# Output projection of a gated hybrid layer: where a weight sum is made, who splits it, and what the merges read

## The chip, the cores and the metric

One NeuronCore of a Trainium2 chip. The metric is the device time of one execution of the whole program, in microseconds (us); several executions are taken and their median is used.

## The reference

One layer on 512 tokens of width 1024, all in float32. A wide input projection feeds two token mixers (a gated linear recurrence and a top-k sparse attention). Only the end of the layer matters here:

```python
ua = einsum('blc,cd->bld', oa * silu(za), w_up_a)      # 512 -> 1024
ub = einsum('blc,cd->bld', ob * silu(zb), w_up_b)      # 512 -> 1024
merged = sigmoid(ga) * ua + sigmoid(gb) * ub
y = einsum('bld,de->ble', merged, w_out)               # 1024 -> 1024
return layer_norm(ALPHA * x + y, ln_g, ln_b)
```

## The kernel before

**Precision.** Every float32 product is made of three matmuls on rounded operands: high by high, high by low, low by high. So every weight tile is loaded by SP's DMA queue, rounded to a high part by ACT (`round_tiles` L965, `split_out_hi` L1213), and the low part, raw minus high, is made by POOL (`split_lo` L1984, `split_out_lo` L2058, a quarter of a weight at a time, 128x512) or in some places by DVE.

**Order of the work.** The program walks units of weights (`UNITS`, L54). A unit is four quarters q, q = 4u to 4u+3, and one quarter is 12 matmuls of 128x512. Units 0 to 26 are the input projection, units 27 to 30 (`up0` to `up3`, q = 108 to 123) the two up projections. Each engine has its own in-order program, written out by quarter: the same q in two engines' loops is only a place in each list, and semaphores tie them. Constants give the places: `T1_AT` and `T1_LO_AT` (DVE), `OUT_HI_AT` (ACT), `OUT_LO_AT` (POOL).

**Up projections and merges.** Two quarters give the two products of 128 channels m (0 to 7), in two of four PSUM banks (`up_bank`). Before a quarter may write its bank again, PE waits until the bank's earlier content was read (`quarter_up`, L717, semaphores `up_out`). `merge(m)` on DVE (L1708) multiplies one bank by its gate into an SBUF tile `mix` (L1719), the other by its gate (L1720), adds the two from SBUF (L1723), waits until ACT has rounded the sum (`round_merged`, L1192), and takes the low part (L1726). After each odd m, `sum_rows` (L1736 to L1743) makes four short differences of 128x256 for the products below, ACT rounds them (`round_sums`, L1197), and DVE makes their low part (`sum_rows_lo`, L1749).

**Output projection.** It is done as a 2x2 block product with seven block products in place of eight. Their weights are, in PE's order (`OUT_WEIGHTS`): `b11`, `b21`, `t1`, `t2`, `b22`, `t3`, `t4`, where t1 = b12 - b11, t2 = b22 - t1, t3 = b22 - b12, t4 = b21 - t2 (`sum_out`, L1770, one DVE instruction of 128x2048 each). Each block product is two passes i of four steps j, three matmuls a step. A step waits for its quarter of the weight's low part (`wait_out_lo`) and, in `b11`, `b21` and `t1`, for the low part of its activations: `b11` step 3 needs merge 6, `b21` step 3 merge 7, `t1` step 3 the last `sum_rows_lo`. `b21` adds to the banks of `b11`, so its pass i waits until ACT has kept a copy (`keep_first`, L1218).

**Where the raw blocks lie.** SP loads `b11` into `z_a` and `b12` into `z_b` behind the weights of `up1`, after `o_lo_done` (both tiles hold branch outputs until then). t1 is written over `b11` in `z_a`, so it waits for `b11`'s low part; its low part is one DVE instruction (`first_sum_lo`, L1776) at q = 121; t2 then overwrites t1, t3 overwrites `b12`. `b21` and `b22` come into the two halves of `w_raw` when the last up weights are split.

**Tail.** DVE adds residuals and partial results in the PSUM banks (`rows_11`, `early_rows`, `rows_12`, `rows_22`), makes the row statistics, and normalises; SP stores the result. `rows_12(i)` frees the banks for `b22`.

Of the kernel before, what the change touches and what calls it, by code (L numbers as in the profile page):

```python
# [93 lines left out]
LO_DVE = tuple(range(Q_PREP[0] // 4 + 1, Q_MERGE // 4 + 2))  # L94
OUT_HI_AT = {109: ((0, 0),), 110: ((0, 1),), 117: ((1, 0),), 118: ((1, 1),), 120: ((2, 0), (2, 1))}
OUT_LO_AT = {110: 0, 119: 1}
T1_AT, T1_LO_AT = 115, 121
ON_POOL = ((), (1,), (1,), ())
# [16 lines left out]
def hybrid_kernel(nc, x_t, x_tok, w_units, w_kiwi, b_cols, b_ia, b_vb, lb_cols, g_cols, rel_bias,  # L115
                  ln_g, ln_b, one_hot, ident, causal, tree_masks, out):
    with ExitStack() as ctx:
# [355 lines left out]
        def out_raw(name):  # L473

            u2, u3 = UNITS.index("up2"), UNITS.index("up3")
            ring = {"b21": u2, "t4": u2, "b22": u3}
            if name in ring:
                return w_raw[:, ring[name] % 2, :].rearrange("p (j n) -> p j n", j=PAIRS)
            return z_a[:] if name in ("b11", "t1", "t2") else z_b[:]

# [6 lines left out]

        LO_ORDER = (0, 1, 4, 3, 5, 6)

        def wait_out_lo(eng, n, pieces):  # L490

            if n == 2:
                eng.wait_ge(out_lo_dve, 1)
            else:
                eng.wait_ge(out_lo, 4 * LO_ORDER.index(n) + pieces)

# [61 lines left out]
        def _(sp):  # L558
# [20 lines left out]
            sp.dma_start(id_sb[:], ident).then_inc(early_in, 16)  # L579
            def load_out(name):  # L580
                sp.dma_start(out_raw(name), w_units[NMAIN - 1 + OUT_BLOCKS.index(name)]
                             .rearrange("p (j n) -> p j n", j=PAIRS)).then_inc(out_in[name], 16)

            for u in range(2, NMAIN):
                if u >= 3:
                    wait_lo(sp, u - 2, 4)
                for a in range(2):
                    load_half(u, a)
                if u == 3:
                    for dst, src in ((lb[:, 0, :], lb_cols), (g_a[:], g_cols), (causal_sb[:], causal),  # L590
                                     (masks_sb[:], tree_masks), (bias_ia[:], b_ia.partition_broadcast(P)),
                                     (bias_vb[:], b_vb.partition_broadcast(P))):
                        sp.dma_start(dst, src).then_inc(consts_in, 16)
                    sp.wait_ge(table_done, 1)
                    sp.dma_start(t5_row, table[:]).then_inc(row_out, 16)
                if u in (10, 14):
                    both_halves((10, 14).index(u))
                if u == 5:
                    sp.wait_ge(row_out, 16)
                    slid = bass.AP(t5_row.tensor, t5_row.offset, [[1, P], [T5W, HEADS_B], [1, 2 * P]])  # L600
                    sp.dma_start(t5_turned[:], slid).then_inc(t5_in, 16)
                if UNITS[u] == "up1":
                    sp.wait_ge(o_lo_done, 4)
                    load_out("b11")
                    load_out("b12")
            sp.wait_ge(recur_done, HEADS_A)
            sp.dma_start(ln_gb[:, 0, :], ln_g.partition_broadcast(P)).then_inc(ln_in, 16)
            sp.dma_start(ln_gb[:, 1, :], ln_b.partition_broadcast(P)).then_inc(ln_in, 16)
            wait_lo(sp, UNITS.index("up2"), 4)
            load_out("b21")  # L610
            wait_lo(sp, UNITS.index("up3"), 4)
            load_out("b22")
            sp.wait_ge(part_done, parts(UNITS.index("up3"), 1))
# [11 lines left out]
        def _(pe):  # L625
# [91 lines left out]
            def quarter_up(u, i, j):  # L717

                fill = 2 * (2 * int(UNITS[u][2]) + i) + j
                if fill < 2:  # L720
                    wait_log_out(pe, TREE0 + 2 * NTREE - 2 + fill)
                    pe.wait_ge(o_hi_done, 2 * (j + 1))
                    pe.wait_ge(o_lo_done, 2 * (j + 1))
                elif fill < 4:
                    wait_turn_out(pe, len(ITEMS) + HEADS_A - 4 + fill)
                else:
                    pe.wait_ge(up_out[fill % 4], fill // 4)
                c = slice(i * P, i * P + P)
# [199 lines left out]
            for n, i in OUT_ORDER:  # L928
# [9 lines left out]
                elif name == "t2":  # L938
                    pe.wait_ge(up_out[i], 2 * KT // 4)
                elif name == "t3":  # L940
# [22 lines left out]
        def _(act):  # L963
# [256 lines left out]
            def move_u(i):  # L1220

                act.wait_ge(up_out[2 + i], 2 * KT // 4)
                act.wait_ge(u_done, i + 1)
                nc.scalar.activation(c21_bank[i][:], u_sum[:, i, :], ACT.Copy).then_inc(u_moved, 1)
# [82 lines left out]
            for q in range(4 * NMAIN):  # L1307
# [39 lines left out]
                if m is not None:  # L1347
                    round_merged(m)
                    if m % 2:
                        round_sums(m // 2)  # L1350
            split_out_hi(4, 0)
            split_out_hi(4, 1)
            round_merged(KT - 1)
            keep_first(0)
            round_sums(PAIRS - 1)
            keep_first(1)
            for n in (3, 5, 6):
# [13 lines left out]
        def _(dve):  # L1371
# [336 lines left out]
            def merge(m):  # L1708
# [43 lines left out]
            def sum_out(name):  # L1752

                dst = out_raw(name)
                if name == "t1":
                    wait_out_raw(dve, "b11")
                    wait_out_raw(dve, "b12")
                    wait_out_lo(dve, 0, 4)
                    a, b = out_raw("b12"), out_raw("b11")
                elif name == "t2":  # L1760
                    wait_out_raw(dve, "b22")
                    dve.wait_ge(out_lo_dve, 1)
                    a, b = out_raw("b22"), out_raw("t1")
                elif name == "t3":
                    a, b = out_raw("b22"), out_raw("b12")
                else:
# [205 lines left out]
        def _(pool):  # L1972
# [95 lines left out]
            for q in range(4 * NMAIN):  # L2068
                side(q)
                if q in OUT_LO_AT:  # L2070
                    for piece in range(4):
                        split_out_lo(OUT_LO_AT[q], piece)
            for n in LO_ORDER[2:]:
                for piece in range(4):
# [75 lines left out]
```

## Time and profile before

| | |
|---|---|
| three executions | median 463.41 us (463.39 to 463.68) |
| the profiled execution | 463.86 us, its span 461.9 us, 1.96 us around it |
| busy share of the span | PE 97%, DVE 69%, ACT 51%, POOL 40% |
| mean granted TensorE clock | 0.988 of full speed |
| chain that ended last | PE 84%, DVE 9%, POOL 2%, ACT 2% |

All times of the profile count from the span's start. A row of a timeline has start, duration, engine, line and operation, output<-inputs with their shapes, the number merged into it, and in brackets the engine's idle time before it and what ended it. A matmul's own duration overlaps with the next one's: read PE by the distance of the starts. `bank` is a PSUM tile, all other names are in SBUF.

### The profile page before, as it was taken

To read this page: it belongs to the slowest core of one execution; us is meant where nothing else is said; L and a number is where in the kernel's file an instruction comes from. 1 tells how busy PE (TensorE), PEld (TensorE's weight loads), DVE (VectorE), ACT (ScalarE), POOL (GpSimd) and SP (SyncE) were. 2 spreads that over 40 slices of the span, in tenths; PEclk is the share of its full clock that TensorE was granted. 3 is DMA by queue.
4 is the path that set the end of the run, shared out by engine and by line. 5 is a ranking of instruction groups with operands and counts; after the bars stand their busy time and mean duration, and the time that the engine had idled before them with its cause. 6 is when DMAs were issued, how large, how long until landed. Compare 5 with 4: busy or idle time off the path is not lost.

```text
span 461.9 us, 7700 instructions
## 1 busy us (share of the span) xinstructions
PE 448.9 (97%) x2946; PEld 365.5 (79%) x2946; DVE 319.4 (69%) x585; ACT 236.7 (51%) x398; POOL 185.3 (40%) x173
## 2 busy tenths in 40 slices
PE   9999999999999999999999999999999999979993
PEld 7778888888888888888888887887888888757782
DVE  4446589999999843447989975960720079789977
ACT  5735454263346655376697485725873523534421
POOL 0444442582259724571013000000074486535972
PEclk9999999999999999999999999999999999988998
DMA  8808222266024620214020312050136352240013
GB/s 265 285 17 291 74 76 92 91 159 206 0 92 106 172 88 1 92 27 157 1 92 3 122 67 89 3 184 0 58 125 258 107 182 93 91 180 3 0 45 136
DMA packets 16724, 47.73 MB, mean 103 GB/s; under 512 B 2441, under 2 KB 4273, under 8 KB 16177
## 3 DMA queue, kind: packets, MB, share of 16 engines
q1 hardware_dynamic: 16448, 47.05, 30.6%
q8 instruction: 23, 0.38, 0.3%
q10 hardware_dynamic: 240, 0.20, 0.2%
q14 instruction: 13, 0.10, 0.1%
HBM read 43.04 MB, written 2.11 MB: 98 GB/s over the span
## 4 chain that ended last, share of the span: by engine, by line
PE 84%; DVE 9%; POOL 2%; issue 2%; ACT 2%; DVEq 0%; POOLq 0%
PE bank L627 21%; PE bank L628 21%; PE bank L629 20%; PE bank L788 2%; PE bank L773 2%; POOL w_lo L2058 2%; PE bank L871 2%; PE bank L824 2%; DVE s_lo L1749 1%; DVE z_a L1770 1%; DVE mix L1723 1%; PE bank L764 1%; PE bank L763 1%; PE bank L954 1%; PE bank L957 1%
## 5 line engine op out<-in xcount | busy, mean ns | idle before, releaser
L1984 POOL TENSOR_TENSOR w_lo<-w_raw,w_hi 128x512 fp32r<-128x512 f32 x84 | 113.1, 1373 | 160.0 <-ACT w_hi L965 160.0
L627 PE MATMUL bank<-x_hi,w_hi 128*128 128x512 f32 x336 | 133.0, 396 | 0.0
L628 PE MATMUL bank<-x_lo,w_hi 128*128 128x512 f32 x336 | 131.2, 390 | 0.0
L629 PE MATMUL bank<-x_hi,w_lo 128*128 128x512 f32 x336 | 130.9, 390 | 0.0
L627 PEld LDWEIGHTS bank<-x_hi,w_hi 128*128 128x128 f32 x336 | 63.1, 188 | 13.9 <-issue 0.8
L629 PEld LDWEIGHTS bank<-x_hi,w_lo 128*128 128x128 f32 x336 | 63.1, 188 | 13.6
L628 PEld LDWEIGHTS bank<-x_lo,w_hi 128*128 128x128 f32 x336 | 63.1, 188 | 12.1
L965 ACT ACTIVATE w_hi<-w_raw 128x1024 fp32r<-128x1024 f32 (+2 forms) x63 | 62.4, 1011 | 7.2 <-PE bank L629 4.1
L1052 ACT ACTIVATE prob<-prob,nmax 128x128 f32<-128x128 f32 (+3 forms) x32 | 17.7, 555 | 41.5 <-DVE nmax L1505 41.5
L1481 DVE MAX8 best<-score 128x8 f32<-128x256 f32 (+2 forms) x48 | 26.8, 559 | 1.0
L1493 DVE COPY prob_t<-bank 128x128 f32<-128x128 f32 (+3 forms) x32 | 14.2, 486 | 19.0 <-PE bank L773 18.9
L1482 DVE MATCH_REPLACE8 score<-best,score 128x256 f32<-128x256 f32 (+2 forms) x48 | 26.0, 543 | 0.0
L627 PE MATMUL bank<-o_hi,w_hi 128*128 128x512 f32 x64 | 25.1, 393 | 0.8 <-DVE mix L1719 0.8
L627 PE MATMUL bank<-w_hi,x_hi 128*128 128x512 f32 x64 | 25.3, 395 | 0.0
L629 PE MATMUL bank<-w_hi,x_lo 128*128 128x512 f32 x64 | 25.0, 390 | 0.0
L628 PE MATMUL bank<-w_lo,x_hi 128*128 128x512 f32 x64 | 24.9, 390 | 0.0
L629 PE MATMUL bank<-o_hi,w_lo 128*128 128x512 f32 x64 | 24.9, 389 | 0.0
L628 PE MATMUL bank<-o_lo,w_hi 128*128 128x512 f32 x64 | 24.9, 389 | 0.0
L1719 DVE TENSOR_TENSOR mix<-bank,gate_a_hi 128x512 f32<-128x512 f32 x4 | 2.7, 686 | 31.7 <-PE bank L629 31.7
L1042 ACT ACTIVATE relus<-bank 128x256 f32<-128x256 f32 (+2 forms) x24 | 10.5, 490 | 21.0 <-PE bank L753 21.0
L2002 POOL TENSOR_TENSOR logit<-t,pen 128x256 f32<-128x256 f32 x24 | 17.4, 742 | 9.1 <-DVE nmax L1505 9.1
L1471 DVE SCALAR_TENSOR_TENSOR score<-relus,w_idx,score 128x256 f32<-128x256 f32 (+2 forms) x21 | 15.6, 744 | 7.7 <-ACT relus L1042 6.0
(269 smaller groups left out, 846.6 us busy)
## 6 DMA issues: line engine op xcount, KB each, us to landing
w_raw<-in_w_units SPq DMA_DIRECT2D x58, 512.0 KB, 4.6
w_raw<-in_w_units SPq DMA_DIRECT2D x2, 1024.0 KB, 4.7
y_sb<-in_x_tok SPq DMA_DIRECT2D x4, 512.0 KB, 4.9
out<-y_sb SPq DMA_DIRECT2D x8, 256.0 KB, 2.0
x_raw_hi<-in_x_t SPq DMA_DIRECT2D x4, 256.0 KB, 4.5
x_raw_lo<-in_x_t SPq DMA_DIRECT2D x4, 256.0 KB, 6.4
t_turned<-t_row SPq DMA_DIRECT2D x1, 1024.0 KB, 9.8
q_hi_g<-q_hi_g SPq DMA_DIRECT2D x8, 128.0 KB, 3.7
```

The source lines that it names most:

```text
L627: nc.tensor.matmul(dst, a_hi, b_hi, start=first, stop=False)
L628: nc.tensor.matmul(dst, a_hi, b_lo, start=False, stop=False)
L629: return nc.tensor.matmul(dst, a_lo, b_hi, start=False, stop=last)
L965: nc.scalar.activation(split_target(u, kiwi_hi, x_hi, w_hi)[:, k, :], raw(u)[:, k, :], ACT.Copy).then_inc(done, 1)
L1042: nc.scalar.activation(relus[:, i % 2, 0:n], log_bank[i % 2][:, 0:n], ACT.Relu, scale=QSCALE).then_inc(log_out[i % 2], 1)
L1052: nc.scalar.activation(prob[:, i % 4, 0:n], prob[:, i % 4, 0:n], ACT.Exp, bias=nmax[:, i % 4:i % 4 + 1], scale=-1.0, accum_out=prob_sum[:, ...
L1471: ins = nc.vector.scalar_tensor_tensor(out=score[b][:], in0=relus[:, i % 2, 0:n], scalar=w, in1=score[b][:], op0=ALU.mult, op1=ALU.add)
L1481: link(nc.vector.max(best8[:], score[b][:]))
L1482: link(nc.vector.match_replace(score[b][:], best8[:], score[b][:], TAKEN))
L1493: nc.vector.tensor_copy(prob_t[:, i % 4, 0:n], turn_bank[i % 2][:, 0:n]).then_inc(turn_out[i % 2], 1)
L1984: nc.gpsimd.tensor_tensor(split_target(u, kiwi_lo, x_lo, w_lo)[:, k, :], raw(u)[:, k, :], split_target(u, kiwi_hi, x_hi, w_hi)[:, k, :].bi ...
L2002: nc.gpsimd.tensor_tensor(logit[:, i % 2, n - band:n], t5[:, h, 2 * P - band:], pen[b][:, n - band:] if b else causal_sb[:], ALU.add).then ...
```

## The change

- t1 is made at q = 106 (T1_AT 115 before), ahead of the up projections. For that SP loads `b11` and `b12` ahead of the weights of `up0`, t1 goes into `z_b` over `b12`, and SP loads `b12` once more, into `z_a`, when `b11`'s low part is there.
- t1's low part is made half by DVE, half by POOL (two pieces behind `b21`'s at q = 121).
- `merge` writes its first product back into its PSUM bank, and the add reads it there. PE's next writer of that bank waits for the add (`mix_done`) in place of the first multiply.
- ACT rounds merge 4 before the two halves of `b21`, and keeps both `b11` copies before the last `round_sums`.

```diff
-OUT_HI_AT = {109: ((0, 0),), 110: ((0, 1),), 117: ((1, 0),), 118: ((1, 1),), 120: ((2, 0), (2, 1))}
-OUT_LO_AT = {110: 0, 119: 1}
-T1_AT, T1_LO_AT = 115, 121
+OUT_HI_AT = {109: ((0, 0),), 110: ((0, 1),), 120: ((2, 0), (2, 1))}
+OUT_HI_THEN = {118: ((1, 0), (1, 1))}
+OUT_LO_AT = {110: ((0, 0), (0, 1), (0, 2), (0, 3)), 119: ((1, 0), (1, 1), (1, 2), (1, 3)), 121: ((2, 2), (2, 3))}
+T1_AT, T1_LO_AT = 106, 121
...
-            return z_a[:] if name in ("b11", "t1", "t2") else z_b[:]
+            return z_a[:] if name in ("b11", "t3") else z_b[:]
...
             for u in range(2, NMAIN):
+                if UNITS[u] == "up0":
+                    sp.wait_ge(o_lo_done, 4)
+                    load_out("b11", z_a[:])
+                    load_out("b12", z_b[:])
                 if u >= 3:
                     wait_lo(sp, u - 2, 4)
...
-                if UNITS[u] == "up1":
-                    sp.wait_ge(o_lo_done, 4)
-                    load_out("b11")
-                    load_out("b12")
...
+            wait_out_lo(sp, 0, 4)
+            sp.wait_ge(out_sum, 1)
+            load_out("b12", z_a[:])
             wait_lo(sp, UNITS.index("up2"), 4)
...
-                else:
-                    pe.wait_ge(up_out[fill % 4], fill // 4)
+                elif fill % 2:
+                    pe.wait_ge(up_out[fill % 4], fill // 4)
+                else:
+                    pe.wait_ge(mix_done, fill // 2 - 1)
...
-                    pe.wait_ge(up_out[i], 2 * KT // 4)
+                    pe.wait_ge(mix_done, KT)
+                    pe.wait_ge(up_out[1], 2 * KT // 4)
...
+                for n, half in OUT_HI_THEN.get(q, ()):
+                    split_out_hi(n, half)
...
             keep_first(0)
+            keep_first(1)
             round_sums(PAIRS - 1)
-            keep_first(1)
...
-                nc.vector.tensor_tensor(mx, up_bank[fa][:], gate_tiles(m, 1)[:, 0, :], ALU.mult).then_inc(up_out[fa], 1)
+                a_gated = up_bank[fa][:]
+                nc.vector.tensor_tensor(a_gated, a_gated, gate_tiles(m, 1)[:, 0, :], ALU.mult).then_inc(a_done, 1)
                 nc.vector.tensor_tensor(gb, up_bank[fb][:], gb, ALU.mult).then_inc(up_out[fb], 1)
-                dve.wait_ge(up_out[fa], m // 2 + 1)
+                dve.wait_ge(a_done, m + 1)
                 dve.wait_ge(up_out[fb], m // 2 + 1)
-                nc.vector.tensor_tensor(mx, mx, gb, ALU.add).then_inc(mix_done, 1)
+                nc.vector.tensor_tensor(mx, a_gated, gb, ALU.add).then_inc(mix_done, 1)
...
                 if name == "t1":
-                    wait_out_lo(dve, 0, 4)
-                    a, b = out_raw("b12"), out_raw("b11")
+                    a, b = z_b[:], z_a[:]
                 elif name == "t2":
                     wait_out_raw(dve, "b22")
-                    dve.wait_ge(out_lo_dve, 1)
-                    a, b = out_raw("b22"), out_raw("t1")
+                    wait_out_lo(dve, 2, 4)
+                    a, b = out_raw("b22"), z_b[:]
...
-                hi, lo = out_weights(2)
-                nc.vector.tensor_tensor(lo, out_raw("t1"), hi.bitcast(F32), ALU.subtract).then_inc(out_lo_dve, 1)
+                hi, lo = (w[:, 0:2, :] for w in out_weights(2))
+                nc.vector.tensor_tensor(lo, out_raw("t1")[:, 0:2, :], hi.bitcast(F32),
+                                        ALU.subtract).then_inc(out_lo_dve, 1)
...
-            for n in LO_ORDER[2:]:
+            for n in LO_ORDER[3:]:
                 for piece in range(4):
                     split_out_lo(n, piece)
```

## Rows read from the trace of the kernel before

**Rows 1.** Who waited for whom, engine PE, whole span: us, times, longest.

```profile
PE bank L954 <- DVE even_lo L1726: 2.8, 1, 2.8
PE bank L627 <- DVE mix L1719: 0.8, 1, 0.8
PE bank L954 <- ACT first_sum L1218: 0.6, 1, 0.6
PE bank L954 <- POOL w_lo L2058: 0.3, 1, 0.3
```

**Rows 2.** Timeline of PE from 403 us to the first step of t2.

```profile
403.04 0.50 PE L627 MATMUL bank<-o_hi,w_hi 128*128 128x512 f32 x1 [0.85 <-DVE mix L1719]
...
409.76 0.39 PE L957 MATMUL bank<-x_hi,even_lo 128*128 128x512 f32 x1
...
410.44 0.39 PE L957 MATMUL bank<-x_hi,even_lo 128*128 128x512 f32 x1
413.65 0.80 PE L954 MATMUL bank<-x_hi,even_hi 128*128 128x512 f32 x1 [2.83 <-DVE even_lo L1726]
...
414.67 0.63 PE L957 MATMUL bank<-x_hi,even_lo 128*128 128x512 f32 x1
415.10 0.63 PE L954 MATMUL bank<-x_hi,even_hi 128*128 128x512 f32 x1
...
431.83 0.39 PE L954 MATMUL bank<-w_hi,s_hi_hi 128*128 128x512 f32 x1
```

**Rows 3.** Stretches: busy and count by engine, PEclk (granted clock), DMA share, GB/s.

```profile
412.90:413.10 0.20, 0.00 (x0) 0.00 (x0) 0.00 (x0) 0.20 (x2) 0.00 (x0) 0.64 1.11 287
...
419.60:419.80 0.20, 0.20 (x2) 0.10 (x2) 0.20 (x1) 0.00 (x0) 0.20 (x1) 0.54 0.00 0
```

**Rows 4.** Timeline of DVE from 336 us to its last instruction.

```profile
336.77 1.75 DVE L1704 TENSOR_TENSOR o_lo<-z_b,o_hi 128x1024 fp32r<-128x1024 f32 x1 [0.48 <-ACT o_hi L1337]
...
369.34 0.69 DVE L1719 TENSOR_TENSOR mix<-bank,gate_a_hi 128x512 f32<-128x512 f32 x1 [30.83 <-PE bank L629]
...
378.49 1.50 DVE L1736 TENSOR_TENSOR s_raw<-mix 128x256 f32<-128x256 f32 x1
379.92 0.41 DVE L1737 TENSOR_TENSOR s_raw<-mix 128x256 f32<-128x256 f32 x1
...
386.98 3.37 DVE L1770 TENSOR_TENSOR z_a<-z_b,z_a 128x2048 f32<-128x2048 f32 x1
...
399.48 0.67 DVE L1726 TENSOR_TENSOR even_lo<-mix,even_hi 128x256 fp32r<-128x256 f32 x1 [2.28 <-ACT even_hi L1192]
...
403.69 1.63 DVE L1723 TENSOR_TENSOR mix<-mix,g_b 128x512 f32<-128x512 f32 x1
...
408.41 2.29 DVE L1776 TENSOR_TENSOR w_lo<-z_a,w_hi 128x2048 fp32r<-128x2048 f32 x1
...
410.61 0.69 DVE L1719 TENSOR_TENSOR mix<-bank,gate_a_lo 128x512 f32<-128x512 f32 x1
...
412.00 0.69 DVE L1723 TENSOR_TENSOR mix<-mix,g_b 128x512 f32<-128x512 f32 x1
...
414.65 0.69 DVE L1719 TENSOR_TENSOR mix<-bank,gate_a_lo 128x512 f32<-128x512 f32 x1
...
421.82 2.28 DVE L1770 TENSOR_TENSOR z_a<-w_raw,z_a 128x2048 f32<-128x2048 f32 x1
...
449.16 0.70 DVE L1817 TENSOR_TENSOR bank<-bank,y_sb 128x512 f32<-128x512 f32 x1 [0.76 <-PE bank L957]
...
458.33 0.75 DVE L1829 SCALAR_TENSOR_TENSOR y_sb<-bank,rstd,ln_gb 128x512 f32<-128x512 f32 x1
```

**Rows 5.** Timeline of POOL, the low parts of b21 and of t2.

```profile
399.82 6.65 POOL L2058 TENSOR_TENSOR x_lo<-w_raw,x_hi 128x512 fp32r<-128x512 f32 x4
...
425.29 9.13 POOL L2058 TENSOR_TENSOR w_lo<-z_a,w_hi 128x512 fp32r<-128x512 f32 x4 [4.79 <-ACT w_hi L1213]
```

**Rows 6.** DMA issues from 320 us on: KB each, median us to landing.

```profile
z_b<-in_w_units SPq DMA_DIRECT2D x1, 1024.0 KB, 9.1
```

More of the change, by code:

```diff
@@ L298, in hybrid_kernel @@
         out_sum, out_hi, out_lo, out_lo_dve = (sem(n) for n in ("out_sum", "out_hi", "out_lo", "out_lo_dve"))
+        a_done = sem("a_done")
         first_kept, pre_12, pre_21 = sem("first_kept"), sem("pre_12"), sem("pre_21")
@@ L486, in wait_out_raw @@
                 eng.wait_ge(out_sum, ("t1", "t2", "t3", "t4").index(name) + 1)
-        LO_ORDER = (0, 1, 4, 3, 5, 6)
+        LO_ORDER = (0, 1, 2, 4, 3, 5, 6)
         def wait_out_lo(eng, n, pieces):
+            before = 4 * LO_ORDER.index(n) - 2 * (LO_ORDER.index(n) > LO_ORDER.index(2))
             if n == 2:
                 eng.wait_ge(out_lo_dve, 1)
+                if pieces > 2:
+                    eng.wait_ge(out_lo, before + pieces - 2)
             else:
-                eng.wait_ge(out_lo, 4 * LO_ORDER.index(n) + pieces)
+                eng.wait_ge(out_lo, before + pieces)
         HI_ORDER = (0, 1, 2, 4, 3, 5, 6)
@@ L579, in _, with load_out @@
             sp.dma_start(id_sb[:], ident).then_inc(early_in, 16)
-            def load_out(name):
-                sp.dma_start(out_raw(name), w_units[NMAIN - 1 + OUT_BLOCKS.index(name)]
+            def load_out(name, dst):
+                sp.dma_start(dst, w_units[NMAIN - 1 + OUT_BLOCKS.index(name)]
                              .rearrange("p (j n) -> p j n", j=PAIRS)).then_inc(out_in[name], 16)
             for u in range(2, NMAIN):
+                if UNITS[u] == "up0":
+                    sp.wait_ge(o_lo_done, 4)
+                    load_out("b11", z_a[:])
+                    load_out("b12", z_b[:])
                 if u >= 3:
@@ L608, in _ @@
             sp.dma_start(ln_gb[:, 1, :], ln_b.partition_broadcast(P)).then_inc(ln_in, 16)
+            wait_out_lo(sp, 0, 4)
+            sp.wait_ge(out_sum, 1)
+            load_out("b12", z_a[:])
             wait_lo(sp, UNITS.index("up2"), 4)
-            load_out("b21")
+            load_out("b21", out_raw("b21"))
             wait_lo(sp, UNITS.index("up3"), 4)
-            load_out("b22")
+            load_out("b22", out_raw("b22"))
             sp.wait_ge(part_done, parts(UNITS.index("up3"), 1))
@@ L1220, in move_u @@
             def move_u(i):
-                act.wait_ge(up_out[2 + i], 2 * KT // 4)
                 act.wait_ge(u_done, i + 1)
@@ L1757, in sum_out @@
                     wait_out_raw(dve, "b12")
-                    wait_out_lo(dve, 0, 4)
-                    a, b = out_raw("b12"), out_raw("b11")
+                    a, b = z_b[:], z_a[:]
                 elif name == "t2":
                     wait_out_raw(dve, "b22")
-                    dve.wait_ge(out_lo_dve, 1)
-                    a, b = out_raw("b22"), out_raw("t1")
+                    wait_out_lo(dve, 2, 4)
+                    a, b = out_raw("b22"), z_b[:]
                 elif name == "t3":
-                    a, b = out_raw("b22"), out_raw("b12")
+                    dve.wait_ge(out_in["b12"], 32)
+                    a, b = out_raw("b22"), z_a[:]
                 else:
@@ L2069, in _ @@
                 side(q)
-                if q in OUT_LO_AT:
-                    for piece in range(4):
-                        split_out_lo(OUT_LO_AT[q], piece)
-            for n in LO_ORDER[2:]:
+                for n, piece in OUT_LO_AT.get(q, ()):
+                    split_out_lo(n, piece)
+            for n in LO_ORDER[3:]:
                 for piece in range(4):
```

## The prediction, made before the changed kernel was run

> **What bounds the kernel now.** I read the busy shares first: PE is busy 97% of the span, so the only time to win is what PE loses. PE's waits [rows 1] say where: except at the start, all lie behind 401 us, in the last up projection and the output projection. In PE's timeline [rows 2] three matmuls take 0.68 us (409.76 to 410.44), one 0.227. Against that distance I count the losses: 1.1 us around 403.04, where a bank waits for merge 5's first multiply (0.1 of it a hiccup before); 3.0 us before 413.65, where `b11` step 3 waits for the low part of merge 6; 0.8 and 0.4 us where `b21` waits for ACT's second copy and `t2` for POOL's low part [rows 1]. The long wait also lowers the clock: it is granted in full until 412.9, stands at half (1.2 of 2.4 GHz) from 413.1, and comes back at 419.8 [rows 3]. PE runs 15 matmuls in there at 0.43 us (414.67 to 415.10, [rows 2]): 15 x 0.2 = 3.0 us. Together 8.3 us of PE time, and no change here can win more.
>
> Why is merge 6 late? Its products are there at 369.3 + 6 x 5.44 = 401.9 (merge 0 starts at 369.34 straight behind PE, two quarters are 24 matmuls or 5.44 us), and DVE begins it at 410.61 [rows 4]. DVE is 8.7 us behind, so from merge 2 to the sum t2 its queue is the bound, with ACT and POOL woven in. The end hangs on DVE too: from the last residual step behind `t3` (449.16) DVE runs without a gap until 459.08 [rows 4], and the store follows. That part isn't touched; it starts when PE has done `t3`. So the gain is what PE reaches `t3`'s end earlier.
>
> **One mechanism prices most steps.** The same 128x2048 subtraction takes 3.37 us at 386.98 and 2.28 at 421.82; the add from two SBUF tiles takes 1.63 at 403.69 and 0.69 at 412.00; a 128x256 step takes 1.50 at 378.49 and 0.41 right behind it [rows 4]. The slow ones are those that start while POOL is inside a piece. Steps with one input in PSUM are 0.69 throughout. I read it as a lock: a DVE step with two SBUF inputs waits out POOL's piece, up to 1.09 us, and POOL waits out DVE's step. While both have work they alternate.
>
> **DVE's queue up to merge 6, term by term.**
> - t1's sum leaves: 3.37 less 0.08 of overlap, -3.3 [rows 4]. At q = 106 DVE is idle (30.8 us before 369.34), so there it costs nothing; it may hold a POOL piece by 2.3 us, and the piece belongs to unit 26's weights and ends near 351, and PE takes them from 353.0 on.
> - Merge 4's low part waited 2.28 us for ACT, which had two halves of `b21` ahead of it (row 399.48). Now ACT rounds merge 4 first; the normal wait of some 0.5 and a lock wait of up to 0.7 stay: -1.1.
> - The adds read PSUM and take no lock: merge 5's -0.94 (1.63 against 0.69), merges 0 and 1 -0.8 by letting POOL finish sooner. No more, since merge 2 can't start before its products at 380.2.
> - t1's low part on DVE is halved, 2.29 to about 1.2: -1.1. POOL gets two pieces, 2.5 us.
> - New lock waits. POOL began `b21`'s low part at 399.82 and ended at 406.47 [rows 5], before the short sums of merge 5. DVE now comes to that merge's low part at about 400 and the sums at 401, with POOL still at `b21` and then at t1's pieces until 405: +0.5 for the low part and three of the four sums at 1.09, +3.8.
>
> Sum: -3.3 - 1.1 - 0.94 - 0.8 - 1.1 + 3.8 = -3.4. Merge 6 starts at 407.2 and its low part is there at about 410.0. Merge 7: 414.65 becomes 411.2. Its add stood in a lock wait too (-0.94), half of it comes back at the low part behind it: t2's sum ends 3.9 us earlier, at 420.2 in place of 424.1.
>
> **PE's side, as a second sum.** The wait at 403 goes: merge 5's add ends at about 399.4, and PE wants the bank at 401.9. PE begins `b11` at 407.5 and comes to step 3 at 409.6: a wait of 0.5 us in place of 3.0, too short to lower the clock (the 0.85 us one at 403.04 didn't). `b11` ends at 413.5. Then `b21` waits for `keep_first(0)`, which stands behind merge 7's rounding at 413.5: 0.9 us in place of 0.8. So PE is at `t2` at 425.3, 6.5 us earlier than before (431.8, [rows 2]). But `t2`'s low part is only 3.9 us earlier: POOL's four pieces took 9.13 us, because t3's and t4's sums on DVE come between them [rows 5]. The last piece ends at 430.5, and PE wanted it at 427.3: 3.2 us of waits, the longest, for the third piece, about 2.5. After: 0.5 + 0.9 + 3.2 = 4.6 us lost in place of 8.3: -3.7. The two sums agree, and I take **-3.8 us**: DVE's queue gives 3.9, and what is left over is POOL's `t2` wait.
>
> **Costed at nothing.** The early loads: the two blocks can go out at 338.5, when the last branch part is split (336.77 + 1.75, [rows 4]), and `up0`'s weights land behind them. Before, `b12` landed 9.1 us after issue as the last of 3 MB [rows 6]; so all is there by about 350, and ACT rounds `up0`'s weights in unit 26, which begins at 369.3 - 16.3 = 353.0. The third load (1 MB, about 376 to 381) is wanted by t3's sum at 421; `b21` and `b22` follow it on SP's queue, at 386 and later. The two `ln` loads stand ahead of SP's new wait. PE's waits for `mix_done`: odd quarters keep theirs, and each even one has 2 us or more (above). Writing a product back to PSUM: steps that write a bank (row 449.16, 0.70) cost what the others do. The add from PSUM, in any case, by its nearest rows: 0.69 with a bank as input (410.61), 0.69 without (412.00) [rows 4]; for the read just behind the write I allow 0 to 0.1 us a merge.
>
> A page speaks against this step. The Trainium skill, "VectorE: DVE Perf Modes", section on the TRN2 errata, gives a PSUM source 120 fixed cycles and an SBUF source 58, which would be 0.065 us more for each add, 0.3 us over the five merges on the path (an estimate from that page). The rows above don't agree: both forms take 0.69.
>
> **Rivals.**
> 1. *The wait moves and takes the clock along (28%).* The new wait at `t2`, about 2.5 us, lies between the one that left the clock alone (0.85) and the one before 413.65, in which it fell 2.1 us after PE's last matmul had ended (410.83, [rows 2, 3]). So a fall is near even. It costs 0.2 us a matmul; a spell as long as before is 3.0 us, one of half the length 1.5. The time is -3.8 + 1.5 to 3.0: 461.1 to 462.6 by the runs. Then the gain was in the first stall and half of it is paid again at `t2`.
> 2. *DVE and POOL don't alternate step by step (15%).* After the slow 378.49 the next sum was 0.41, but POOL had just run out of pieces. If only the first sum waits, 2.2 us come back, and with the POOL pieces for `t2` as much again at most: 455.8 to 458.
> 3. *The savings are eaten by lock waits (8%).* The two extra POOL pieces meet DVE where it is densest, and two more waits of 1.09 and a late phase bring merge 6 to its old place: `b11` waits and loses the clock again, 463 to 463.9.
> 4. *Slower: banks held until the add (6%).* The point is the quarter at 401.9, which now waits for merge 5's add and not its first multiply. With DVE as late as before (add ending 405.3) PE stands 3.4 us there, loses the clock (3.0) and begins `b11` at 413.9, when its low part is just ready; the old wait of 3.0 and spell of 3.0 are gone, so it is no change until the add ends after 405.6, and from there every us counts: two lock waits more are +2.2, 465.5. Against it: the add ends at 399.4 by the sum above, 6 us before the point.
>
> That the change does not do what it says is no rival with weight: DVE and SP are idle where t1 is put.
>
> **The numbers.** The profiled execution is 463.86, 0.45 above the median of the runs, 463.41. 463.86 - 3.8 = 460.1 for a profiled one; against the median 459.6. The forecast's own chance is 43%, its own range 458.3 to 460.7. The range that holds 8 in 10 reaches from 457.4 (most of rival 2) to 462.5 (rival 1 up to a full spell); rivals 3 and 4 and the far end of 2 are left out. A measurement of this kernel tells apart about 0.2%, 0.93 us. Faster by more: forecast, nearly all of rival 1, rival 2: 0.84. Within: rival 3 and the edge of 1: 0.10. Slower: 0.06.
>
> **What the profile would show.** Right: no PE wait near 403; `b11` step 3 waits under 1 us and the clock stays full around 413; the adds at L1723's place are 0.7 every time; the sums of merge 5 show 1.4 to 1.5 in several of the four steps; merge 6 starts near 407, merge 7 near 411, t2's sum ends near 420; PE's largest wait is `t2` for POOL's low part. Wrong: sums of 0.41 there and merge 6 near 404 (rival 2); half clock near 430 (rival 1); merge 6 after 410 (rival 3); a PE wait for merge 5's add (rival 4). A DVE gap of over 10 us between `t3` and the end would break the step that carries the gain to the end.

## The result and the profile after

The changed kernel takes **460.66 us** (median of 4 executions, 459.87 to 461.21) against 463.43 (463.39 to 463.68): a ratio of 0.9938, 95% interval 0.9921 to 0.9955, so 2.8 us less. The prediction was 459.6, with a range of 457.4 to 462.5 and 0.84 for faster. A second measurement of the same kernel gave 461.57 (6 executions, 0.9944, 0.9927 to 0.9962). The profiled execution took 459.87 us, its span is 457.8 us, 4.1 less than before.

From the page of after: the span, PE's busy share, the granted clock in 40 slices.

```profile
span 457.8 us, 7703 instructions
...
PE 445.2 (97%) x2946; PEld 362.8 (79%) x2946; DVE 319.7 (70%) x585; ACT 236.7 (52%) x398; POOL 186.3 (41%) x175
...
PEclk9999999999999999999999999999999999999997
```

Only the last slice, behind the matmuls, is below full clock. Who waited for whom on PE, after (us, times, longest), answering to [rows 1]:

```profile
PE bank L965 <- POOL w_lo L2072: 2.6, 2, 2.3
...
PE bank L965 <- DVE even_lo L1739: 1.0, 1, 1.0
PE bank L965 <- ACT first_sum L1229: 0.5, 1, 0.5
```

The largest wait has changed its place: not `b11` for DVE's low part of merge 6 (2.8 before), but `t2` for POOL. The wait at 403 is gone. PE's timeline of after, answering to [rows 2]:

```profile
409.96 0.50 PE L965 MATMUL bank<-x_hi,even_hi 128*128 128x512 f32 x1 [0.98 <-DVE even_lo L1739]
...
414.23 0.50 PE L965 MATMUL bank<-x_hi,odd_hi 128*128 128x512 f32 x1 [0.54 <-ACT first_sum L1229]
...
425.24 0.39 PE L965 MATMUL bank<-w_hi,s_hi_hi 128*128 128x512 f32 x1
...
429.07 0.50 PE L965 MATMUL bank<-w_hi,s_hi_lo 128*128 128x512 f32 x1 [2.28 <-POOL w_lo L2072]
...
430.32 0.50 PE L965 MATMUL bank<-w_hi,s_hi_lo 128*128 128x512 f32 x1 [0.29 <-POOL w_lo L2072]
```

`t2` begins at 425.24 in place of 431.83, 6.6 us earlier, and gives 2.6 back at once. The chain of work that ended last passes this place in both kernels: it comes from DVE over `t2`'s four low parts on POOL to PE's matmul behind the last of them, at 430.32 here. Before, that matmul was (POOL's row in [rows 5] ends at 434.42)

```profile
434.47 0.50 PE L954 MATMUL bank<-w_hi,s_hi_lo 128*128 128x512 f32 x1 [0.27 <-POOL w_lo L2058]
```

PE's wait at `b11` and its half clock before are not in that chain: PE came to `t2`'s last piece 0.27 us too early even so.

DVE's timeline of after, answering to [rows 4]:

```profile
345.36 2.74 DVE L1783 TENSOR_TENSOR z_b<-z_b,z_a 128x2048 f32<-128x2048 f32 x1 [7.30 <-DMA z_b<-in_w_units]
368.89 0.70 DVE L1732 TENSOR_TENSOR bank<-bank,gate_a_hi 128x512 f32<-128x512 f32 x1 [20.79 <-PE bank L637]
...
398.21 0.69 DVE L1736 TENSOR_TENSOR mix<-bank,g_b 128x512 f32<-128x512 f32 x1
399.60 1.51 DVE L1739 TENSOR_TENSOR odd_lo<-mix,odd_hi 128x512 fp32r<-128x512 f32 x1 [0.70 <-ACT odd_hi L1203]
401.04 1.50 DVE L1749 TENSOR_TENSOR s_raw<-mix 128x256 f32<-128x256 f32 x1
402.47 1.51 DVE L1750 TENSOR_TENSOR s_raw<-mix 128x256 f32<-128x256 f32 x1
403.90 1.51 DVE L1753 TENSOR_TENSOR s_raw<-s_raw,mix 128x256 f32<-128x256 f32 x1
405.44 0.43 DVE L1756 TENSOR_TENSOR s_raw<-mix,s_raw 128x256 f32<-128x256 f32 x1
405.78 1.22 DVE L1789 TENSOR_TENSOR w_lo<-z_b,w_hi 128x1024 fp32r<-128x1024 f32 x1
406.92 0.69 DVE L1732 TENSOR_TENSOR bank<-bank,gate_a_lo 128x512 f32<-128x512 f32 x1
...
410.95 0.69 DVE L1732 TENSOR_TENSOR bank<-bank,gate_a_lo 128x512 f32<-128x512 f32 x1
...
417.71 2.28 DVE L1783 TENSOR_TENSOR z_b<-w_raw,z_b 128x2048 f32<-128x2048 f32 x1
...
445.04 0.70 DVE L1831 TENSOR_TENSOR bank<-bank,y_sb 128x512 f32<-128x512 f32 x1 [0.76 <-PE bank L968]
...
454.21 0.75 DVE L1843 SCALAR_TENSOR_TENSOR y_sb<-bank,rstd,ln_gb 128x512 f32<-128x512 f32 x1
```

The adds are 0.69 throughout, and three of merge 5's four short sums take 1.5 us, though a sum of this size takes 0.41: I read it as alternation with POOL (experiment 6 tests it). POOL's rows for the low parts of `b21`, t1's two pieces and t2 [rows 5] are now

```profile
395.79 6.47 POOL L2072 TENSOR_TENSOR x_lo<-w_raw,x_hi 128x512 fp32r<-128x512 f32 x4
402.22 2.90 POOL L2072 TENSOR_TENSOR w_lo<-z_b,w_hi 128x512 fp32r<-128x512 f32 x2
...
421.17 9.10 POOL L2072 TENSOR_TENSOR w_lo<-z_b,w_hi 128x512 fp32r<-128x512 f32 x4 [4.79 <-ACT w_hi L1224]
```

**One offset first.** Merge 0 begins at 369.34 before and at 368.89 after. Among the twelve profiles of this study it lies between 368.39 and 369.44, and in two profiles of the changed kernel alone it is 368.89 and 369.30. So I don't count the 0.45 of the 4.1 us as the edit's, and below I count DVE's times from merge 0. Counted so, they repeat within 0.02 us in the two profiles of the changed kernel, up to where PE's clock differs (431 us).

### The profile page after: what moved, and what is told of

It is laid out like the page before. It is cut to its first block, busy times and chain, and to the rows that moved or that the text cites. A ratio compares the mean times of both kernels' runs of the same rounds, so it can differ in the third digit from the quotient of the medians.

```text
span 457.8 us, 7703 instructions
## 1 busy us (share of the span) xinstructions
PE 445.2 (97%) x2946; PEld 362.8 (79%) x2946; DVE 319.7 (70%) x585; ACT 236.7 (52%) x398; POOL 186.3 (41%) x175
## 4 chain that ended last, share of the span: by engine, by line
PE 85%; DVE 9%; POOL 2%; issue 2%; ACT 2%; DVEq 0%; POOLq 0%
PE bank L635 21%; PE bank L636 21%; PE bank L637 21%; PE bank L798 2%; PE bank L783 2%; POOL w_lo L2072 2%; PE bank L881 2%; PE bank L834 2%; DVE s_lo L1762 1%; PE bank L774 1%; PE bank L773 1%; PE bank L965 1%; PE bank L968 1%; PE bank L967 1%; PE bank L925 1%
## 5 line engine op out<-in xcount | busy, mean ns | idle before, releaser
L1697 DVE TENSOR_TENSOR w_lo<-w_raw,w_hi 128x512 fp32r<-128x512 f32 x32 | 20.6, 684 | 0.0
```

The lines of the kernel that those rows point to most:

```text
L1697: nc.vector.tensor_tensor(split_target(u, kiwi_lo, x_lo, w_lo)[:, k, :], raw(u)[:, k, :], split_target(u, kiwi_hi, x_hi, w_hi)[:, k, :].bi ...
```

## The experiments

My theory, after this reading: the gain comes from DVE's queue up to merge 6, which PE's order then follows; the lock between DVE and POOL (a DVE step with two inputs in SBUF and a POOL piece exclude each other) sets both the three slow sums and the late third piece of t2; and the median is above the profiled execution because the clock falls in PE's wait at `t2` in some executions. The rivals: that the early sum t1 alone did it; that the add from PSUM is worth only its own 0.94 us; that sharing t1's low part pays.

Places in each profile, in us from merge 0, worked out from the timelines: the start of DVE's merges 3, 5 and 6, the end of t2's sum on DVE, the start of PE's last matmul; then merge 5's four short sums, and where the profile shows the clock at half ahead of the last matmul:

| kernel | merge 3 | merge 5 | merge 6 | t2 sum | last matmul | merge 5's sums | half clock |
|---|---|---|---|---|---|---|---|
| before | 20.93 | 32.97 | 41.27 | 54.76 | 84.76 | 0.41 0.41 0.41 0.42 | at `b11` |
| after | 17.04 | 27.94 | 38.03 | 51.10 | 81.09 | 1.50 1.51 1.51 0.43 | none |
| `after_again` | 17.05 | 27.93 | 38.02 | 51.10 | 82.38 | 1.51 1.51 1.51 0.43 | at `t2` |
| `sbuf_add` | 17.62 | 29.36 | 39.91 | 53.41 | 83.36 | 1.51 1.51 1.51 0.43 | none |
| `t1_late` | 19.24 | 30.03 | 40.12 | 53.20 | 84.08 | 1.50 1.51 1.51 0.42 | at `t2` |
| `pool_hold` | 17.03 | 27.93 | 35.83 | 48.92 | 78.87 | 1.51 0.41 0.41 0.42 | none |
| `lo_on_dve` | 17.03 | 27.93 | 36.89 | 49.96 | 81.52 | 1.50 0.41 0.41 0.42 | at `t2` |
| `before_psum_add` | 19.24 | 31.28 | 39.13 | 52.19 | 82.18 | 0.41 0.41 0.41 0.43 | none |
| `before_act_order` | 20.94 | 31.73 | 41.14 | 54.64 | 84.60 | 1.51 0.41 0.41 0.42 | at `b11` |
| `rows_first` | 17.03 | 27.95 | 38.04 | 51.10 | 78.96 | 1.51 1.51 1.51 0.42 | none |
| `both` | 17.03 | 27.95 | 35.86 | 48.96 | 76.78 | 1.50 0.41 0.41 0.42 | none |
| `lo_rows` | 17.05 | 27.94 | 36.90 | 49.97 | 77.83 | 1.50 0.41 0.41 0.42 | none |

One regularity is worth more than the medians. From the end of t2's sum to the last matmul it takes 29.95 to 30.00 us in six profiles, whatever PE waited for at `b11` and `b21`, and whether or not the clock fell at `b11`. Where the clock fell at `t2` it takes 0.9 to 1.6 more (31.28, 30.88, 31.56), and in the three kernels with the rows first 27.82 to 27.86. So a part of the change is worth what it does to t2's sum, and a fall of the clock costs time at `t2` and none at `b11`.

**1. `after_again`: the changed kernel once more.**

> The changed kernel once more, unaltered, to see its spread. Theory A (the gain is 3.7 to 4.1 us with the clock full throughout, and in some executions the clock falls in the 2.3 us wait ahead of t2's third quarter and up to 2 us are given back): 459.6 to 461.4 again, a spread of over 0.8 us where before has 0.3, and if the profile falls on a slow one it shows half clock near 430 us. Rival B (the spread comes from the early part of the kernel, as loads): a slow profile shows full clock near 430 and merge 0 later than 369.4.

Six executions: 459.55, 459.72, 461.55, 461.59, 461.83, 461.99, with nothing between; the upper four are up to 0.6 above the expected range. The profiled one is 461.55. Stretches of it: busy time and count of PE, PEld, DVE, ACT, POOL, then the granted clock, DMA share and GB/s; then PE's timeline.

```profile
429.00:429.50 0.50, 0.01 (x1) 0.02 (x1) 0.50 (x1) 0.50 (x2) 0.50 (x2) 1.00 0.00 0
430.00:430.50 0.50, 0.50 (x2) 0.01 (x1) 0.47 (x2) 0.34 (x1) 0.50 (x1) 0.71 0.00 0
431.00:432.00 1.00, 1.00 (x3) 0.81 (x4) 0.97 (x3) 0.00 (x0) 1.00 (x2) 0.50 0.00 0
433.50:434.00 0.50, 0.50 (x4) 0.41 (x3) 0.34 (x1) 0.24 (x1) 0.50 (x1) 0.88 0.00 0
```

```profile
429.49 0.49 PE L965 MATMUL bank<-w_hi,s_hi_lo 128*128 128x512 f32 x1 [2.26 <-POOL w_lo L2072]
...
430.73 0.79 PE L965 MATMUL bank<-w_hi,s_hi_lo 128*128 128x512 f32 x1 [0.19 <-POOL w_lo L2072]
...
433.45 0.47 PE L965 MATMUL bank<-w_hi,s_hi_hi 128*128 128x512 f32 x1
...
451.68 0.39 PE L968 MATMUL bank<-x_hi,odd_lo 128*128 128x512 f32 x1
```

The wait is the same to 0.02 us (2.26 here, 2.28 in the first profile), but here the clock stands at 1.2 of 2.4 GHz from about 430.2 to 433.6, and there it stays full. The first profile's stretch, and its last matmul, are

```profile
431.00:432.00 1.00, 1.00 (x6) 0.82 (x5) 0.97 (x3) 0.00 (x0) 1.00 (x2) 1.00 0.00 0
...
449.98 0.39 PE L968 MATMUL bank<-x_hi,odd_lo 128*128 128x512 f32 x1
```

From the third piece to the last matmul PE needs 22.19 us here (451.68 - 429.49) and 20.91 there (449.98 - 429.07): the fall costs 1.28 us. So rival 1's mechanism and the forecast's are both true, of different executions of one program. For the executions without a profile only the mean clock is on record: 0.990 to 0.991 in three of the upper four, 0.994 in the fourth (461.59), in both of the lower ones and in all of the first set (459.87 to 461.21). It doesn't settle them, since a fall at the end of the program, where no matmul is left, lowers the mean as well. That the fall makes the whole spread is therefore not shown.

**2. `sbuf_add`: the change without the adds from PSUM.**

> The changed kernel with the merges adding from SBUF again, PE waiting for the first multiply. Theory A (an add from SBUF waits out a POOL piece, up to 1.09 us, and holds POOL off): merge 5's add ends 2.4 us later, near 401, merge 6's low part near 411.4, t2's sum 2.4 us later near 422.4: 462.5 to 463.2, b11's wait 2.6 us in place of 1.0, the clock perhaps down there. Rival (the lock wait only changes places, since POOL's pieces are the same number): within 0.5 us of the changed kernel, 460.2 to 461.2.

```diff
-                a_gated = up_bank[fa][:]
-                nc.vector.tensor_tensor(a_gated, a_gated, gate_tiles(m, 1)[:, 0, :], ALU.mult).then_inc(a_done, 1)
+                nc.vector.tensor_tensor(mx, up_bank[fa][:], gate_tiles(m, 1)[:, 0, :], ALU.mult).then_inc(up_out[fa], 1)
...
-                nc.vector.tensor_tensor(mx, a_gated, gb, ALU.add).then_inc(mix_done, 1)
+                nc.vector.tensor_tensor(mx, mx, gb, ALU.add).then_inc(mix_done, 1)
```

(and the waits of PE, ACT and DVE as they were before the change). 462.91 us (12 executions, 461.70 to 464.27; 0.9988, 0.9976 to 1.0001), as expected: most of the gain is gone. Merge 5 in its timeline:

```profile
400.00 1.65 DVE L1733 TENSOR_TENSOR mix<-mix,g_b 128x512 f32<-128x512 f32 x1
402.35 1.01 DVE L1736 TENSOR_TENSOR odd_lo<-mix,odd_hi 128x512 fp32r<-128x512 f32 x1 [0.70 <-ACT odd_hi L1200]
```

The add is held 0.96, and in turn holds POOL, so the low part behind it gets 0.50 back. Merge 6 is 1.88 later than in after, t2's sum 2.31, and PE waits 2.9 at `b11` again.

**3. `before_psum_add`: the kernel before with that part alone.** The same edit the other way round.

> The kernel before with one part of the change: the merges keep the first product in its PSUM bank, add from there, and PE waits for the add. Theory A (each add then takes no lock and doesn't hold POOL): merge 6's low part 2.3 us earlier, b11's wait 1.2 us in place of 2.8 and the clock up there, t2's sum 2.8 us earlier: 460.8 to 461.8, single executions up to 463 where the clock falls at t2. Rival (the adds gain only the two slow ones on the path, 1.9 us, and the clock still falls at b11): 462 to 463. Rival (PE's wait for the add costs more than the lock): 463.6 or more, with a longer PE wait near 402.

461.34 us (5 executions, 460.94 to 461.82; 0.9953, 0.994 to 0.9966): -2.25, nearly all that the whole change brings. Merge 6 comes 2.14 earlier and t2's sum ends 2.57 earlier. That is far more than one add's 0.94: t1's sum too takes 2.28 here in place of 3.37, because POOL is done sooner, so part of what the forecast booked under t1's sum comes with the adds. The wait before `b11` step 3 is 0.9 in place of 2.8, and the clock stays full there; but the last matmul comes 2.58 earlier, just as much as t2's sum, so the clock adds nothing to it. PE's waits (first and third of the view):

```profile
PE bank L958 <- ACT first_sum L1222: 2.7, 2, 2.2
...
PE bank L958 <- DVE even_lo L1730: 0.9, 1, 0.9
```

and in ACT's timeline the reason for the first:

```profile
419.42 1.06 ACT L1201 ACTIVATE s_hi_lo<-s_raw 128x1024 fp32r<-128x1024 f32 x1 [3.64 <-DVE s_raw L1747]
420.38 0.58 ACT L1222 ACTIVATE first_sum<-bank 128x512 f32<-128x512 f32 x1
```

The second copy of `b11` stands behind the rounding of the last sums, and PE waits 2.16 us for it. In the changed kernel, which has `keep_first(1)` ahead, that wait is gone; but no time hangs on it here, since PE then still waits 0.30 at `t2` for POOL.

**4. `before_act_order`: the kernel before with ACT's order of the change alone.**

```diff
-OUT_HI_AT = {109: ((0, 0),), 110: ((0, 1),), 117: ((1, 0),), 118: ((1, 1),), 120: ((2, 0), (2, 1))}
+OUT_HI_AT = {109: ((0, 0),), 110: ((0, 1),), 120: ((2, 0), (2, 1))}
+OUT_HI_THEN = {118: ((1, 0), (1, 1))}
...
+                for n, half in OUT_HI_THEN.get(q, ()):
+                    split_out_hi(n, half)
...
             keep_first(0)
+            keep_first(1)
             round_sums(PAIRS - 1)
-            keep_first(1)
```

> The kernel before with another part alone: ACT rounds merge 4 ahead of b21's halves, and keeps both b11 copies ahead of the last rounding of sums. Theory A (DVE then comes 1.7 us earlier to merge 5, but meets POOL's b21 pieces, and gives it all back in lock waits): 463.0 to 463.7, no change; merge 6 starts at 410.2 to 410.6. Rival (it gives its 1.1 us and the 0.8 of b21): 461.5 to 462.3.

463.31 us (12 executions, 462.77 to 465.21, three of them above 464.8; 1.0001, 0.999 to 1.0012): nothing. Merge 5 does begin 1.24 earlier (32.97 to 31.73), as the step had it (-1.1); but DVE then meets POOL still inside `b21`'s pieces, one short sum takes 1.51 in place of 0.41, merge 6 is 0.13 earlier, and t2's sum 0.12. What the three slow executions had, no profile shows. Time won in front of a lock is spent at it.

**5. `t1_late`: the change with t1's sum at its old place.** One edit: `T1_AT` 115 in place of 106.

> The changed kernel with t1's sum back at q = 115, between the merges; all else stays. Theory A (DVE is behind there, but part of the 2.2 us is slack before merge 4 and 5): t2's sum ends 1.9 us later, 461.7 to 462.6, b11's wait about 2.5 us. Rival (the early sum is the whole gain, 3.3 us): 463.4 or more. Rival (DVE's queue there is hidden): 460.7.

462.98 us (12 executions, 461.91 to 464.18; 0.9986, 0.9976 to 0.9996): 0.4 above the range, so a miss. The sum itself is quick there:

```profile
386.19 2.28 DVE L1783 TENSOR_TENSOR z_b<-z_b,z_a 128x2048 f32<-128x2048 f32 x1
```

2.28 us in place of 3.37 before, and merge 6 is 2.09 later than in after. What I had left out is the clock: PE waits 3.02 for merge 6, where it stays full, and 2.28 at `t2`, where the profile has it at half at 432 to 433. That fall costs 0.9 (30.88 us from t2's sum to the last matmul, for 30.0), and 463.12 less 0.9 would be in the range. The spread is 2.3 us, but the mean clocks of the executions (0.987 to 0.994) don't order their times, so what makes it isn't settled.

**6. `pool_hold`: POOL's pieces of t1's low part wait until the sums of merge 5 are made.**

```diff
             def split_out_lo(n, piece):
 
+                if n == 2:
+                    pool.wait_ge(s_raw_done, 12)
                 name = OUT_WEIGHTS[n]
```

> The changed kernel with POOL's two pieces of t1's low part held back until DVE has made the four short sums of merge 5. Theory A (those pieces cost DVE two lock waits of 1.09 us, and they aren't wanted before 419): two of the three 1.5 us sums at 401 to 405 shrink to 0.4, merge 6 starts near 404.9, b11 does not wait, t2's sum ends near 417.9: 2.1 us faster than the changed kernel, 458.2 to 459.2. Rival (the sums wait for POOL whatever is in its queue, or POOL is then late for t1): no gain, 460.2 to 461.5.

457.95 us (4 executions, 457.71 to 458.24; 0.9878, 0.9865 to 0.989), 0.25 better than the expected range. DVE's and POOL's rows:

```profile
401.58 1.51 DVE L1749 TENSOR_TENSOR s_raw<-mix 128x256 f32<-128x256 f32 x1
403.01 0.41 DVE L1750 TENSOR_TENSOR s_raw<-mix 128x256 f32<-128x256 f32 x1
403.34 0.41 DVE L1753 TENSOR_TENSOR s_raw<-s_raw,mix 128x256 f32<-128x256 f32 x1
```

```profile
404.29 3.46 POOL L2074 TENSOR_TENSOR w_lo<-z_b,w_hi 128x512 fp32r<-128x512 f32 x2 [1.49 <-DVE s_raw L1756]
```

Two sums went from 1.51 to 0.41, 2.20 together, and merge 6 is 2.20 earlier; up to merge 5 nothing moved (27.93 for 27.94). POOL stood idle for 1.49 and nobody needed its pieces. This is the lock by itself, with its price: 1.10 us for each of the two sums that met a piece.

**7. `lo_on_dve`: t1's low part wholly on DVE, in one 128x2048 step.** The kernel after with POOL's two pieces left out and the DVE step over all of `w_lo`.

> The changed kernel with t1's low part made by DVE alone again, as in the kernel before. Theory A (sharing it costs more than it gives: POOL's two pieces cost two lock waits of 1.09 us and save 1.1 us of DVE): merge 6 starts 1 us earlier, near 405.9, b11 waits under 0.3 us, t2's sum 1 us earlier: 458.9 in executions without a fall of the clock, median 458.7 to 460.5. Rival (the share pays, as it frees DVE by 1.1 us): 461.2 to 462.5.

460.08 us (5 executions, 459.31 to 460.55; 0.9924, 0.9913 to 0.9936). The DVE step is 2.28 in place of 1.22, two sums 0.41 in place of 1.51: -2.20 + 1.06 = -1.14, and the table has merge 6 at 36.89 for 38.03. So the sharing that the change brings in costs more than it saves. The clock falls at `t2` in its profile (460.55) and costs 1.6; the two executions with a mean clock of 0.994 are 459.31 and 459.75, the three at 0.991 are 460.08 to 460.55. Without a fall I had expected 458.9, so the lowest is 0.4 above that.

**8. `rows_first`: DVE's statistics and early residual steps ahead of the sums t3 and t4.** The wait left in all kernels built on the change is `t2` for POOL, whose four pieces take 9.1 us because t3's and t4's sums come between. This kernel puts other DVE work there.

```diff
-            sum_out("t3")
             dve.wait_ge(ln_in, 32)
             rows_11(0)
-            sum_out("t4")
             rows_11(1)
             early_rows(0)
+            sum_out("t3")
+            rows_12(0)
             early_rows(1)
-            rows_12(0)
             rows_12(1)
+            sum_out("t4")
```

(on ACT, `move_u` goes ahead of the rounding of t4).

> The changed kernel with DVE's order behind t2's sum altered: the two b21 row steps and the first of t1's ahead of t3's sum, and t4's sum behind rows_12; ACT moves the partial sums ahead of rounding t4. Theory A (t2's low part on POOL is late only because t3's and t4's sums come between its pieces): the four pieces take about 5 us in place of 9.1, PE's 2.3 us wait at t2 goes, and with it the falls of the clock: 456.3 to 457.5, spread under 0.5 us. Rival (DVE's work there is a bound of its own and t4's sum is now late): 458.5 to 460.5, with a new PE wait at b22 or t4.

457.90 us (4 executions, 457.70 to 458.00; 0.9878, 0.9865 to 0.9891). The pieces now run without a hold, and PE's waits have no POOL at `t2`:

```profile
421.15 5.04 POOL L2074 TENSOR_TENSOR w_lo<-z_b,w_hi 128x512 fp32r<-128x512 f32 x4 [4.79 <-ACT w_hi L1224]
```

```profile
PE bank L965 <- DVE even_lo L1741: 1.0, 1, 1.0
PE bank L965 <- DVE bank L1803: 0.7, 1, 0.7
```

From t2's sum to the last matmul it is 27.86 us in place of 29.99. The time is 0.4 above the expected range: t4's sum (3.23 at 432.23) now stands ahead of `b22`'s statistics, DVE waits 0.93 for `rstd` behind ACT's rounding of t4, and PE 0.7 for a partial bank. The spread of these four is 0.3 us; but in `pool_hold`, which keeps a wait of 2.19 at `t2`, it is 0.5, so that the missing wait is what narrows it is not shown.

**9. `both`: 6 and 8 together.**

> Both rearrangements of the kernel after at once: GpSimd's pieces of t1's low part held back until DVE has made all the sums for b21, b22 and b12, and DVE's statistics and early rows ahead of the sums of t3 and t4. If the two savings lie at different places of the path (lock alternation ahead of merge 6, the wait for t2's third piece behind b21), they add up: each kernel alone measured 457.95 and 457.90, against 459.6 of the kernel after where its clock does not fall, so 1.65 and 1.7 off, together 3.35 off: 455.9 to 456.7. Rival: the earlier merges only lengthen the two new waits of the second part (0.9 on DVE for the normalisation's row behind ScalarE's rounding of t4, 0.7 on PE for the last partial bank), and the second saving is used up: 457.2 to 457.9.

**455.99 us** (5 executions, 455.68 to 456.51; 0.9843, 0.9829 to 0.9856), 7.2 below the kernel before, as added up. PE's waits are down to two, the first of them at the program's start:

```profile
PE bank L925 <- POOL eps L1991: 1.1, 1, 1.1
PE bank L965 <- DVE bank L1803: 0.7, 1, 0.7
```

and from 420 to 445 us the clock is full and PE busy for 24.28 of 25.00:

```profile
420.00:445.00 25.00, 24.28 (x108) 19.78 (x107) 23.52 (x30) 7.27 (x14) 19.02 (x14) 1.00 0.05 21
```

The two savings lie at different places and add (t2's sum at 48.96, and 27.82 behind it), so the rival (the second used up by the first) is out.

**10. `lo_rows`: 7 and 8 together.**

> T1's low part wholly on DVE (nothing of it on GpSimd) together with the statistics and early rows ahead of the sums of t3 and t4. If GpSimd's part of t1's low part costs the path by the lock steps it forces on DVE, this takes it away as the hold does, less the longer DVE instruction (2 more pieces): merge 6 0.5 to 1.0 earlier than in the kernel after, and with the other saving 456.4 to 457.4. Rival: if the sharing does pay, 457.9 or more, which is what the rows alone measured.

456.86 us (4 executions, 456.46 to 457.12; 0.986, 0.9847 to 0.9874): in the range, 1.0 below the rows alone and 0.9 above `both`, in the order of merge 6 (1.13 and 2.17 earlier than in after).

## Why the prediction was right, and where it was off

**The mechanism was right, down to the number of slow sums.** DVE's terms, before against after, from merge 0:

| term | forecast | measured |
|---|---|---|
| merges 0 and 1 (merge 2's start 11.70 to 11.12) | -0.8 | -0.58 |
| t1's sum gone (rest of merge 3's start) | -3.3 | -3.31 |
| from merge 3 to merge 4 (4.85 to 4.95) | 0 | +0.10 |
| merge 4 no more behind `b21` on ACT (merge 4 to 5, 7.19 to 5.95) | -1.1 | -1.24 |
| merge 5's add, 1.63 to 0.69 | -0.94 | -0.94 |
| t1's low part, 2.29 to 1.22 | -1.1 | -1.07 |
| lock waits: `odd_lo` 1.00 to 1.51, three sums at 1.09 to 1.10 | +3.8 | +3.8 |
| merge 6 | -3.4 | -3.24 |
| t2's sum ends | -3.9 | -3.66 |

- *Rival 2* (no alternation) is out: three sums of 1.5. `pool_hold` shows what its world would be, 1.7 us below the lower group of after.
- *Rival 4* did not come: no wait near 403, merge 5's add ended at 398.9, some 3 us ahead of 401.9, when PE wanted the bank.
- *Rival 3*, savings eaten by lock waits, came for one part alone (ACT's order, experiment 4), but not for the whole.
- *The early loads at nothing*: right. t1's sum waited for its DMA (idle 7.30) and ran at 345.36; the POOL pieces it met took 7.09 us in place of 5.05, and nobody on PE waited.
- *Writing back to PSUM and reading it*: no cost, 0.69 in all eight adds, 0.78 us from the second multiply's start to the add's, and 0.79 before (411.21 to 412.00). The Trainium skill, "VectorE: DVE Perf Modes", section on the TRN2 errata, would have an add from PSUM 0.065 us dearer by the estimate in the prediction; the rows don't agree.

**PE's side.** Lost to waits: 0.98 at `b11` (forecast 0.5), 0.54 at `b21` (0.9), 2.6 at `t2` (3.2), the longest for its third piece as forecast, 2.28 (about 2.5). `t2` began at 425.24 (425.3), but 0.45 of that is the offset, so counted from merge 0 it was 0.4 late. From before to after PE's last matmul is at 449.98 for 454.10, -4.12, less the offset 0.45: **-3.67 against -3.7**. DVE's last stretch without a gap begins at 445.04 in place of 449.16 and is 9.9 us long in both. The forecast for a profiled execution was 460.1, the first profiled one 459.87.

**But the two sums of the prediction are one sum.** It let PE's losses (8.3 before, 4.6 after) confirm DVE's -3.9. Both counts of PE end at the last piece of `t2`'s low part, which DVE's and POOL's chain sets, so they had to agree. The 3.0 of half clock and the wait at `b11` were by themselves no time that a change could win: with the fall (before, `before_act_order`) and without it (`before_psum_add`) the last matmul comes 29.96 to 30.00 us after t2's sum. The times of the kernel before say much the same. Of its 49 executions in the three later sets, seven have a mean clock of 0.988, as the profile with its long spell has, and five have 0.997 or more, which leaves no room for such a spell; their medians are 463.79 and 463.11. Those 0.7 us, and not 3.0, go with the clock, and no profile shows where.

**Where it was off: the median.** The step at fault takes the forecast's world (43%) for the time of the kernel, with rival 1 as another world of 28%. The fall of the clock at `t2` is no property of the kernel but of an execution: it came in the second profile and not in the first, behind the same wait. The lower group of the second set (459.55, 459.72) is the forecast's 459.6; the upper four (461.55 to 461.99) are in rival 1's range (461.1 to 462.6), though only one of them has a profile. The median lies where most executions do, in the first set between, in the second at 461.57. The size of the rival was high as well: 1.5 to 3.0 for the fall, 1.28 measured, since it ended 2.7 us after the matmuls had got going slow (430.73 to 433.45), against 15 slow matmuls in [rows 2, 3]. Between the two profiled executions (459.87 and 461.55) the 1.28 of the fall and the 0.41 by which merge 0 begins later (368.89, 369.30) make the whole difference. Between the groups of the second set, 2.1 apart, 0.8 is left over and has no profile to explain it. Open too is whether the 460.51 to 461.21 of the first set are falls. So the clock as the cause of the median's 1.1 us above the forecast is shown for one execution and argued for the rest. Why the kernel before spreads less (0.3 in the first set, 1.3 over 23 executions in the second) is in part clear: the fall in its profile was at `b11`, where no time hung on PE, and the changed kernel's is at `t2`, behind which PE is the bound.

**What the parts are worth.** By what they do to the end of t2's sum: the adds from PSUM 2.57 alone (2.25 in the medians), and 2.31 as the last part added; t1's early sum 2.10 as the last part added; ACT's order 0.12 alone, and once merge 6 is early it removes a wait of 2.16 at `b21`, on which no time hung in experiment 3. Sharing t1's low part costs 1.14; it is the only part that works against the change. The parts overlap, since a shorter queue on DVE also changes which POOL piece each step meets, so they don't add up to 3.66.

## What to carry to other kernels

If two engines take turns at a lock, price every step by whether it meets the other engine's piece: moving work to a helper can cost more than it carries (here two pieces of help, 1.06 us saved, cost two waits of 1.10). Short steps suffer most (0.41 becomes 1.51), so keep the helper's pieces out of their stretch, by a wait on the helper if need be, and give the contended stretch the steps that don't take the lock. Where a forecast leaves the matmul engine a wait like the one here, 2.3 us with the matmul engine as the bound behind it, forecast two times, with and without a fallen clock. And before you book a wait of the matmul engine as time to win, follow the chain that ended last: here 2.8 us of wait and 3.0 of half clock at `b11` were worth nothing, because a later wait for another engine took up whatever PE won.

## What the runs showed of the hardware that I had not expected

- **The lock takes turns by the single step.** Each of DVE's steps in a row (`odd_lo` and three sums) waited once, as if POOL had got one piece in between each. The price was 1.1 us for a step of 0.41 and for one of 2.28 [rows 4], and less for steps that came when the piece was further on (0.96 for merge 5's add in `sbuf_add`, 0.82 for `odd_lo`, 1.51 for 0.69). The Trainium skill, "SBUF — State Buffer", section on the two separate sides, has the lock as exclusive and held for a whole instruction, between a GpSimd instruction and a DVE one with two SBUF inputs; the rows agree (POOL's four pieces 5.04 free, 9.10 with sums between them).
- **A step that pays at the lock shortens the next.** A held add (1.65) left the low part behind it at 1.01, a free one (0.69) at 1.51: so 0.96 saved is 0.46 by itself, and more only through what POOL does earlier.
- **The clock's fall is a draw.** Waits of 2.26 (fell), 2.28 (didn't) and 2.27 (fell, `lo_on_dve`, whose stretch is below); in `pool_hold`'s profile 2.19, full clock. In the waits of 2.83 before and 3.83 in `before_act_order` at `b11` it fell, though five other executions of the kernel before have too high a mean clock for that spell.

```profile
430.00:431.00 1.00, 1.00 (x4) 0.70 (x4) 0.96 (x2) 0.00 (x0) 1.00 (x2) 0.50 0.00 0
```

But the waits of 3.02 in `t1_late` and 2.85 in `sbuf_add` at `b11` left it full in their profiles. So the length of the wait alone does not decide it.
- **The relative times repeat to 0.02 us** between the two profiled executions of the changed kernel, for all that is not PE's clock: here single profiles were enough to settle DVE's part of the question, and only the clock needs many executions.
